# Last unit of expert weights in column halves: left columns first, then the right columns row by row

## The chip, the core and the metric

The kernel runs on one core of a Trainium2 chip. A core has five engines that run side by side: TensorE (PE) for matmuls, VectorE (DVE), ScalarE (ACT), GpSimd (POOL) and SyncE (SP), which here only issues transfers. Sixteen DMA engines move data between the chip's main memory and the core's on-chip memory of 128 partitions. TensorE writes its results into PSUM, eight banks of 512 float32 columns on 128 partitions. Engines wait for one another by semaphores. The metric is the time of one execution on the device in microseconds, here the median of the runs; less is better.

## What is computed

One layer of a decoder over 256 tokens of width 1024: attention and retention mixers side by side, their merge, then a mixture of 32 experts, of which each token uses 4, and a final norm. Only the experts' part matters here:

```python
def expert_block(args):
    tok, e = args
    xb = x_pad[tok]
    gu = xb @ w1[e] + b1[e]
    gate = jnp.minimum(gu[:, :F], SWIGLU_LIMIT)
    up = jnp.clip(gu[:, F:], -SWIGLU_LIMIT, SWIGLU_LIMIT)
    act = (up + 1.0) * gate * jax.nn.sigmoid(SWIGLU_ALPHA * gate)
    return act @ w2[e] + b2[e]
# y = expert output * gate weight, added to each token's row; then
return rmsnorm(x, norm_final_g)
```

w1 is 1024 x 2048 and w2 is 1024 x 1024 for each expert, in float32.

## The kernel before

The kernel loads every expert's weights once, all 32, and that is what most of the time goes to. The weights come in units of 2 MB: four units for w1 (two rows of 128 contracted values each, `W1_ROWS`) and two for w2 (four such rows each, `W2_ROWS`). A ring of ten places holds them. SP issues the loads in the order in which TensorE uses them, each when its place is free (`s_used` counts used units). Each unit's landing has a semaphore, and a transfer adds 16 to it when all 16 engines have done their part.

An expert has 64 slots for tokens (`CAP`). So each matmul of the experts has only 64 result rows, and the kernel puts two of them side by side: columns 0 to 511 of the result on partitions 0 to 63 of PSUM, columns 512 to 1023 on partitions 64 to 127. In `hidden_unit` (line 1241), `down_row` (line 1300) and `last_row` (line 1350) the loop over `c` goes through these halves. The halves of an expert's output are then brought back to token rows by `scatter_tile` (line 1390): for each tile of 128 tokens two matmuls, one that contracts partitions 0 to 63 (left columns) and one that contracts partitions 64 to 127 (right columns), added into banks 4 to 7, which hold the residual.

Weights and activations are float32, and such a matmul is two instructions of TensorE: the trace shows 32 of line 1350 for 16 matmuls. Each has its own weight load, which is listed under PEld.

The main loop handles 30 experts. The last two are written out: `hidden_last` for the hidden layer of expert 31 and `down_last` for the down projections of experts 30 and 31. There, three units of w2 are loaded in halves of two rows (line 574), and the last unit, the second of expert 31, in four quarters of one row (line 578), each with a semaphore of its own (`s_quarter`), so that TensorE can do a row when it has landed. The order on TensorE at the end is:

- rows 0 and 1 of expert 31's first unit of w2 (`down_halves(2, ...)`), then the scatter of token tile 1 of expert 30, then rows 2 and 3
- four rows of the last unit, each behind its own wait; the last adds to `s_used`
- `scatter_last`: the scatter of token tile 0 of expert 30, which needs nothing new, then, when DVE has copied expert 31's output from bank 1 of PSUM (line 1881, `main.ye`), tile 0 and tile 1 of expert 31. These two raise `s_first` and `s_scattered`.

ACT sums the squares of a token tile when these are raised (line 894) and takes the root (line 896); DVE inverts it and scales the tile (line 1907), and SP stores it in four pieces (line 593). Before that, DVE at the end does nothing but the copies from PSUM that the matmuls wait for. The routing of this input leaves no expert with more than 64 tokens, so the blocks for extra work (`If n > 0`) are not entered.

Of the kernel before, what the change touches and what calls it, by code (L numbers as in the profile page):

```python
# [16 lines left out]
P = 128  # L17
D = 1024
# [4 lines left out]
HALF = 512  # L23
# [14 lines left out]
CAP = 64  # L38
# [70 lines left out]
def hybrid_block_kernel(nc, x_in, g_mix, w_in, rel_bias, w_att, w_ret, w_out, g_ffn, w_router, b_router,  # L109
                        w1, b1, w2, b2, g_final, c_early, c_lasting, c_decay, c_onehot, c_mask, c_item,  # L110
                        c_expert, out):
    with ExitStack() as ctx:
# [3 lines left out]
        def sem(name):  # L116
            return ctx.enter_context(nc.semaphore(name))
# [257 lines left out]
        main, extra = Steps("main"), Steps("extra")  # L375
        s_w2half = [sem(f"last_w2_second_half_loaded{n}") for n in range(3)]
        s_first = sem("first_tile_scattered")

        s_unit = [sem(f"ring_unit_loaded{j}") for j in range(RING)]
        s_used = sem("ring_units_used")  # L380
# [14 lines left out]
        def w1_tile(flat):  # L395
            return flat.rearrange("p (j n) -> p j n", j=W1_ROWS)

        def w2_tile(flat):
            return flat.rearrange("p (j n) -> p j n", j=W2_ROWS)

        def w1_source(e, u):
            rows = W1_ROWS * P
            return w1[bass.ds(e, 1), u * rows:(u + 1) * rows, :].rearrange("e (p j) n -> p (e j) n", j=W1_ROWS)
# [11 lines left out]
        def w2_number(e, u):  # L415
            return W1_UNITS + E_UNITS * e + W1_UNITS + u if e < N_EXP - 1 else N_UNITS - W2_UNITS + u

        def place(n):
            in_halves = n >= RING and n % RING < HALF_UNITS
            return ring[n % RING], s_unit[n % RING], 16 * (n // RING + 1 + in_halves)  # L420

        def load_w1(sp, e, u, n):
            flat, landed, _ = place(n)
            sp.dma_start(w1_tile(flat), w1_source(e, u)).then_inc(landed, 16)

        def load_w2(sp, e, u, n):
            flat, landed, _ = place(n)
# [43 lines left out]
        def _(sp):  # L471
# [101 lines left out]
                    rows = slice(h * W2_ROWS // 2, (h + 1) * W2_ROWS // 2)  # L573
                    sp.dma_start(w2_tile(flat)[:, rows, :], w2_source(e, u)[:, rows, :]).then_inc(s_w2half[n] if h else landed, 16)
            sp.wait_ge(s_used, N_UNITS - 1 - RING + 1)
            for j in range(W2_ROWS):
                flat, _, _ = place(N_UNITS - 1)
                sp.dma_start(w2_tile(flat)[:, j, :], w2_source(N_EXP - 1, 1)[:, j, :]).then_inc(s_quarter[j], 16)  # L578

            sp.wait_ge(s_used, N_UNITS)  # L580
            sp.wait_ge(s_table, 1)
# [319 lines left out]
        def _(pe):  # L901
# [442 lines left out]
                        mm = row(flat, u * W2_ROWS + j)  # L1344
                mm.then_inc(s_used, 1)

            def last_row(flat, q):
                for c in range(2):
                    lhs = last_actT[:, (q % 4) * P + (q // 4) * CAP:(q % 4) * P + (q // 4) * CAP + CAP]
                    mm = pe.matmul(ps[CAP * c:CAP * c + CAP, 1, :], lhs,  # L1350
                                   w2_tile(flat)[:, q % W2_ROWS, c * HALF:(c + 1) * HALF],
                                   start=False, stop=(q == FQ - 1))
                return mm

            def down_last():
                i = N_EXP - 1
                down_bias(main, i - 1)
                down_halves(0, i - 1, 0, down_row)
                transpose_slots(main, i - 1)
                pe.wait_ge(main.act, i + 1)  # L1360
                for j in range(4):
                    mm = pe.transpose(ps[:, 0, j * P:(j + 1) * P], act_sb[:, j * P:(j + 1) * P], ident)
                mm.then_inc(main.at, 1)
                down_halves(1, i - 1, 1, down_row)
                pe.wait_ge(main.swe, i + 1)
                transpose_slots(main, i)
                pe.wait_ge(main.sel2, i + 1)
                pe.wait_ge(main.ate, i + 1)
                for c in range(2):
                    pe.matmul(ps[CAP * c:CAP * c + CAP, 1, :], sel2[0:BIAS_ROWS, :],  # L1370
                              bias[:, 2 * F + c * HALF:2 * F + (c + 1) * HALF], start=True, stop=False)
                down_halves(2, i, 0, last_row)
                flat, _, _ = place(w2_number(i, 1))
                for j in range(W2_ROWS):
                    pe.wait_ge(s_quarter[j], 32)
                    mm = last_row(flat, W2_ROWS + j)
                mm.then_inc(s_used, 1)

            def project_down_extra(i):
                down_bias(extra, i)  # L1380
                for u in range(W2_UNITS):
                    pe.wait_ge(s_extra2[u], i * 16 + 16)
                    down_unit(w2_part(u), u).then_inc(extra.w2_used, 1)
                    if u == 0:
                        transpose_slots(extra, i)

            def scatter_tile(t, weights, y):
                for c in range(2):
                    rows = slice(CAP * c, CAP * c + CAP)
                    mm = pe.matmul(bank(4 + 2 * t + c), weights[rows, t * P:(t + 1) * P], y[rows, :], start=False,  # L1390
                                   stop=True, skip_group_check=True)
                return mm

            def scatter(s, i):

# [4 lines left out]
                mm.then_inc(s_scattered, 1)  # L1400

            def scatter_last():
                scatter_tile(0, sc_w, y_sb)
                pe.wait_ge(main.ye, N_EXP + 1)
                pe.wait_ge(main.swe, N_EXP + 1)
                scatter_tile(0, last_sc, last_y).then_inc(s_first, 1)
                scatter_tile(1, last_sc, last_y).then_inc(s_scattered, 1)

            def second_scales():
                pe.wait_ge(main.slots, 2)  # L1410
# [43 lines left out]
        def _(dve):  # L1454
# [422 lines left out]
            store_y(main, N_EXP - 2)  # L1877
            dve.wait_ge(main.sw, N_EXP)
            dve.tensor_copy(last_sc, ps[:, 2, 0:T]).then_inc(main.swe, 1)
            dve.wait_ge(s_used, N_UNITS)  # L1880
            dve.tensor_copy(last_y, bank(1)).then_inc(main.ye, 1)
            n = dve.value_load(list_i[0:1, 0:1], min_val=0, max_val=MAX_EXTRA)
            with dve.If(n > 0):
                dve.wait_ge(s_scattered, N_EXP + 1)
# [54 lines left out]
```

## Time and profile before

| what | us |
|---|---|
| median of three runs | 1231.49 |
| lowest and highest | 1231.02, 1231.54 |
| the profiled execution | 1230.75 |
| its span, first to last instruction | 1228.7 |
| TensorE busy | 1168.7 (95%) |
| DVE busy, ACT busy | 427.1, 206.2 |
| moved by DMA | 462.31 MB, 376 GB/s in the mean |

The profile comes from one execution. Times in its rows count from the first instruction. A "busy" TensorE has at least one matmul in flight; its matmuls overlap, so the mean duration of one is longer than the distance from one to the next. The granted clock of TensorE was full throughout, but for the last slices behind its work.

### The profile page before, as it was taken

The page shows a single profiled execution, that of the slowest core. Times are in us where ns is not written, and L with a number is a line of the kernel's source. Part 1 is how long each engine was busy: PE and PEld are TensorE (multiplying, and loading weights), DVE is VectorE, ACT ScalarE, POOL GpSimd, SP SyncE. Part 2 cuts the span into 40 slices and gives each one's busy share as a digit, 9 for nine tenths or more (in the row PEclk, how much of TensorE's full clock was granted, in tenths as well). Part 3 has the DMA queues.
Part 4 walks back from the last instruction along what each step waited for, and adds up shares of the span by engine and source line. Part 5 has one row for each costly group of instructions (what it writes and reads, how often), then busy time and mean ns, then how long its engine had stood idle before and what let it go on. Part 6 is the DMA issues. An engine that isn't in the chain of part 4 may idle for free.

```text
span 1228.7 us, 17261 instructions
## 1 busy us (share of the span) xinstructions
PE 1168.7 (95%) x7138; PEld 584.6 (48%) x7138; DVE 427.1 (35%) x744; ACT 206.2 (17%) x303; POOL 58.6 (5%) x43
## 2 busy tenths in 40 slices
PE   9999999999999999999999999999999999899997
PEld 8888888888633333333333333333333333333332
DVE  5966765655722232222222222222222222222222
ACT  6444553534400000000000000000000000000001
POOL 0950000000300000000000000000000000000000
PEclk9999999999999999999999999999999999999999
DMA  9856437838999999999999999999999999999996
GB/s 312 267 207 224 152 137 269 310 140 350 409 428 427 429 428 428 428 429 428 429 428 428 429 428 428 428 428 429 429 428 428 429 428 429 428 429 429 428 425 281
DMA packets 57250, 462.31 MB, mean 376 GB/s; under 512 B 5761, under 2 KB 7490, under 8 KB 31906
## 3 DMA queue, kind: packets, MB, share of 16 engines
q1 hardware_dynamic: 53848, 458.97, 90.1%
q10 hardware_dynamic: 3370, 2.88, 0.8%
q8 instruction: 24, 0.39, 0.1%
q14 instruction: 8, 0.07, 0.0%
HBM read 459.71 MB, written 1.07 MB: 375 GB/s over the span
## 4 chain that ended last, share of the span: by engine, by line
PE 59%; DMA 37%; SPq 1%; ACT 1%; DVE 1%; issue 0%; DVEq 0%; ACTq 0%
DMA w_ring<-in_w 23%; PE ps L1241 15%; PE ps L1300 11%; DMA behind_watt<-in_w 7%; DMA behind_xb<-in_w 7%; PE ps L958 4%; PE ps L1390 3%; PE ps L966 3%; PE ps L964 3%; PE ps L965 3%; PE ps L1215 2%; PE ps L959 2%; SPq L578 1%; PE ps L978 1%; PE ps L1091 1%; PE ps L1093 1%
## 5 line engine op out<-in xcount | busy, mean ns | idle before, releaser
L1241 PE MATMUL ps<-w_ring,A_W 128*64 128x512 f32 x1232 | 278.1, 596 | 30.6 <-DMA w_ring<-in_w 29.1
L1830 DVE TENSOR_SCALAR A_W<-ps 128x512 f32<-128x512 f32 x32 | 22.1, 691 | 484.0 <-PE ps L1241 484.0
L1241 PEld LDWEIGHTS ps<-w_ring,A_W 128*64 128x64 f32 x1232 | 85.4, 137 | 205.8 <-issue 149.8
L1300 PE MATMUL ps<-w_ring,A_W 128*64 128x512 f32 x592 | 134.2, 595 | 0.0
L1472 DVE TENSOR_TENSOR w_parts<-w_ring,w_parts 128x1024 fp32r<-128x1024 f32 x76 | 110.0, 1466 | 57.2 <-ACT w_parts L690 56.3
L1241 PE MATMUL ps<-A_QK,A_W 128*64 128x512 f32 x416 | 94.2, 594 | 9.2 <-DMA A_QK<-in_w 8.7
L869 ACT ACTIVATE A_W<-ps 128x512 f32<-128x512 f32 x31 | 18.5, 597 | 438.3 <-PE ps L1281 438.3
L690 ACT ACTIVATE w_parts<-w_ring 128x1024 fp32r<-128x1024 f32 x75 | 78.9, 1058 | 64.7 <-PE ps L959 32.1
L865 ACT ACTIVATE A_W<-A_W 128x512 f32<-128x512 f32 x32 | 20.2, 630 | 394.8 <-DVE A_W L1830 394.8
L958 PE MATMUL ps<-hT_both,w_parts 128*128 128x512 f32 x224 | 79.3, 399 | 0.0
L1300 PEld LDWEIGHTS ps<-w_ring,A_W 128*64 128x64 f32 x592 | 40.4, 136 | 68.6 <-issue 66.9
L964 PE MATMUL ps<-w_parts,hT_both 128*128 128x512 f32 x176 | 69.6, 396 | 0.0
L966 PE MATMUL ps<-w_parts,hT_both 128*128 128x512 f32 x176 | 68.6, 390 | 0.0
L965 PE MATMUL ps<-w_parts,hT_both 128*128 128x512 f32 x176 | 68.5, 389 | 0.0
L1390 PE MATMUL ps<-A_W 64*128 64x512 f32 x264 | 65.9, 616 | 0.0
L959 PE MATMUL ps<-hT_both,w_parts 128*128 128x256 f32 x224 | 62.9, 281 | 0.0
L1241 PEld LDWEIGHTS ps<-A_QK,A_W 128*64 128x64 f32 x416 | 29.3, 137 | 70.4 <-issue 53.1
L1847 DVE COPY A_W<-ps 128x512 f32<-128x512 f32 x31 | 21.4, 692 | 98.2 <-PE ps L1300 98.2
L1241 PE MATMUL ps<-behind_watt,A_W 128*64 128x512 f32 x208 | 47.4, 597 | 5.4 <-DMA behind_watt<-in_w 5.0
L1241 PE MATMUL ps<-behind_xb,A_W 128*64 128x512 f32 x192 | 43.7, 597 | 5.5 <-DMA behind_xb<-in_w 5.0
L1215 PE MATMUL ps<-A_W,x_parts 128*128 128x64 bf16 x1488 | 48.5, 193 | 0.0
L958 PEld LDWEIGHTS ps<-hT_both,w_parts 128*128 128x128 f32 x224 | 42.1, 188 | 11.1 <-issue 0.6
(264 smaller groups left out, 1215.1 us busy)
## 6 DMA issues: line engine op xcount, KB each, us to landing
w_ring<-in_w SPq DMA_DIRECT2D x110, 2048.0 KB, 43.5
A_QK<-in_w SPq DMA_DIRECT2D x38, 2048.0 KB, 42.6
behind_watt<-in_w SPq DMA_DIRECT2D x19, 2048.0 KB, 43.5
w_ring<-in_w_in SPq DMA_DIRECT2D x36, 1024.0 KB, 7.4
behind_xb<-in_w SPq DMA_DIRECT2D x18, 2048.0 KB, 43.5
w_ring<-in_w SPq DMA_DIRECT2D x10, 1024.0 KB, 9.3
w_ring<-in_w_ret_branch SPq DMA_DIRECT2D x2, 2048.0 KB, 10.5
A_W<-in_w_out SPq DMA_DIRECT2D x1, 2560.0 KB, 13.2
```

The costliest lines, as they stand in the source:

```text
L690: act.activation(hi, raw, ACT.Copy).then_inc(s_wh, 1)
L958: pe.matmul(o, wh, tokens_both(k), start=first, stop=False, skip_group_check=True)
L959: mm = pe.matmul(o[:, 0, :], wl, hT_hi[:, k, :], start=False, stop=last, skip_group_check=True)
L964: pe.matmul(bank(b + t), hh, hi, start=first, stop=False)
L965: pe.matmul(bank(b + t), hh, lo, start=False, stop=False)
L966: mm = pe.matmul(bank(b + t), hl, hi, start=False, stop=last)
L1215: mm = pe.matmul(ps[:, 2, k * CAP:(k + 1) * CAP], x_part(part, t)[:, k * P:(k + 1) * P], s_one[:, t, :], start=(part == 0 and t == 0), sto ...
L1241: mm = pe.matmul(o, XT[:, k, :], tile[:, j, c * HALF:(c + 1) * HALF], start=(k == 0), stop=(k == KC - 1))
L1300: mm = pe.matmul(ps[CAP * c:CAP * c + CAP, 3, :], lhs, w2_tile(flat)[:, q % W2_ROWS, c * HALF:(c + 1) * HALF], start=False, stop=(q == FQ ...
L1390: mm = pe.matmul(bank(4 + 2 * t + c), weights[rows, t * P:(t + 1) * P], y[rows, :], start=False, stop=True, skip_group_check=True)
L1472: dve.tensor_tensor(lo, raw, hi.bitcast(F32), ALU.subtract).then_inc(s_wl, 1)
L1830: dve.tensor_scalar(gl, bank(0), LIMIT, None, ALU.min).then_inc(s.g, 1)
```

## The change

The last unit of w2 is still four transfers with four semaphores and the same 2 MB. They are now cut by columns first: the left 512 columns of all four rows (1 MB), then the right 512 columns of rows 0 and 1 (512 KB), of row 2 (256 KB) and of row 3 (256 KB). A partition's piece of a row is thus 2 KB where it was 4 KB.

TensorE does the left columns of all four rows behind the first landing and raises a new semaphore `s_left`. Then it does the scatter of tile 0 of expert 30, which stood behind the last row before. Then come the right columns of rows 0 and 1, and of row 2; the left scatter of expert 31's tile 0, which waits for DVE's copy of the left half; and the right columns of row 3. The sums of the right half go to bank 0 instead of bank 1, so that DVE can copy the left half out of bank 1 while TensorE writes the right one. DVE makes two copies of 64 partitions where it made one of 128. Behind the last row TensorE does the left scatter of tile 1, waits for the second copy, and does the right scatters of tile 0 and tile 1.

```diff
@@ load plan (SP)
+        LAST_PIECES = [(slice(0, W2_ROWS), slice(0, HALF)), (slice(0, 2), slice(HALF, D)),
+                       (slice(2, 3), slice(HALF, D)), (slice(3, 4), slice(HALF, D))]
...
-            for j in range(W2_ROWS):
-                flat, _, _ = place(N_UNITS - 1)
-                sp.dma_start(w2_tile(flat)[:, j, :], w2_source(N_EXP - 1, 1)[:, j, :]).then_inc(s_quarter[j], 16)
+            last_unit, last_source = w2_tile(place(N_UNITS - 1)[0]), w2_source(N_EXP - 1, 1)
+            for n, (rows, cols) in enumerate(LAST_PIECES):
+                sp.dma_start(last_unit[:, rows, cols], last_source[:, rows, cols]).then_inc(s_quarter[n], 16)
@@ TensorE
-            def last_row(flat, q):
-                for c in range(2):
+            def last_bank(c):
+                return ps[CAP * c:CAP * c + CAP, 1 - c, :]
+
+            def last_row(flat, q, columns=range(2)):
+                for c in columns:
                     lhs = last_actT[:, (q % 4) * P + (q // 4) * CAP:(q % 4) * P + (q // 4) * CAP + CAP]
-                    mm = pe.matmul(ps[CAP * c:CAP * c + CAP, 1, :], lhs,
-                                   w2_tile(flat)[:, q % W2_ROWS, c * HALF:(c + 1) * HALF],
+                    mm = pe.matmul(last_bank(c), lhs, w2_tile(flat)[:, q % W2_ROWS, c * HALF:(c + 1) * HALF],
                                    start=False, stop=(q == FQ - 1))
                 return mm
@@ down_last
+                pe.wait_ge(s_quarter[0], 32)
                 for j in range(W2_ROWS):
-                    pe.wait_ge(s_quarter[j], 32)
-                    mm = last_row(flat, W2_ROWS + j)
+                    mm = last_row(flat, W2_ROWS + j, (0,))
+                mm.then_inc(s_left, 1)
+                scatter_tile(0, sc_w, y_sb)
+                for n in range(1, 4):
+                    if n == 3:
+                        pe.wait_ge(main.ye, N_EXP + 1)
+                        pe.wait_ge(main.swe, N_EXP + 1)
+                        scatter_columns(0, 0, last_sc, last_y)
+                    pe.wait_ge(s_quarter[n], 32)
+                    rows = LAST_PIECES[n][0]
+                    for j in range(rows.start, rows.stop):
+                        mm = last_row(flat, W2_ROWS + j, (1,))
                 mm.then_inc(s_used, 1)
@@ scatter
+            def scatter_columns(t, c, weights, y):
+                rows = slice(CAP * c, CAP * c + CAP)
+                return pe.matmul(bank(4 + 2 * t + c), weights[rows, t * P:(t + 1) * P], y[rows, :], start=False,
+                                 stop=True, skip_group_check=True)
...
             def scatter_last():
-                scatter_tile(0, sc_w, y_sb)
-                pe.wait_ge(main.ye, N_EXP + 1)
-                pe.wait_ge(main.swe, N_EXP + 1)
-                scatter_tile(0, last_sc, last_y).then_inc(s_first, 1)
-                scatter_tile(1, last_sc, last_y).then_inc(s_scattered, 1)
+                scatter_columns(1, 0, last_sc, last_y)
+                pe.wait_ge(main.ye, N_EXP + 2)
+                scatter_columns(0, 1, last_sc, last_y).then_inc(s_first, 1)
+                scatter_columns(1, 1, last_sc, last_y).then_inc(s_scattered, 1)
@@ DVE
+            dve.wait_ge(s_left, 1)
+            dve.tensor_copy(last_y[0:CAP, :], ps[0:CAP, 1, :]).then_inc(main.ye, 1)
             dve.wait_ge(s_used, N_UNITS)
-            dve.tensor_copy(last_y, bank(1)).then_inc(main.ye, 1)
+            dve.tensor_copy(last_y[CAP:P, :], ps[CAP:P, 0, :]).then_inc(main.ye, 1)
```

## Rows read from the trace of the kernel before

**Rows 1.** The page: span, busy times, and DMA rate in 40 slices

```profile
span 1228.7 us, 17261 instructions
PE 1168.7 (95%) x7138; PEld 584.6 (48%) x7138; DVE 427.1 (35%) x744; ACT 206.2 (17%) x303; POOL 58.6 (5%) x43
GB/s 312 267 207 224 152 137 269 310 140 350 409 428 427 429 428 428 428 429 428 429 428 428 429 428 428 428 428 429 429 428 428 429 428 429 428 429 429 428 425 281
```

**Rows 2.** Chain that ended last, final stretch: start us, us, what

```profile
1194.79 23.71 DMA w_ring<-in_w
...
1218.54 1.08 PE ps L1350 x4
1219.62 1.95 PE ps L1390 x8
...
1221.59 1.12 ACT w_ring L894 x2
```

**Rows 3.** Timeline from 1210 on: start us, us, engine, line, operation [idle before]

```profile
1210.23 1.94 PE L1350 MATMUL ps<-w_ring,A_W 128*64 128x512 f32 x8
1212.10 1.13 PE L1390 MATMUL ps<-A_W 64*128 64x512 f32 x4
1213.16 4.51 PE L1350 MATMUL ps<-w_ring,A_W 128*64 128x512 f32 x20
1218.54 1.08 PE L1350 MATMUL ps<-w_ring,A_W 128*64 128x512 f32 x4 [0.87 <-DMA w_ring<-in_w]
1219.55 2.85 PE L1390 MATMUL ps<-A_W 64*128 64x512 f32 x12
1219.67 0.69 DVE L1881 COPY A_W<-ps 128x512 f32<-128x512 f32 x1 [8.91 <-PE ps L1350]
1220.41 0.30 PEld L1390 LDWEIGHTS ps<-A_W 64*128 64x128 f32 x4 [0.56 <-DVE A_W L1881]
1221.59 1.02 ACT L894 ACTIVATE w_ring<-ps 128x1024 f32<-128x1024 f32 x1 [13.20 <-PE ps L1390]
1222.94 1.00 ACT L894 ACTIVATE w_ring<-ps 128x1024 f32<-128x1024 f32 x1
```

**Rows 4.** Line 1350 in thin stretches, and its durations in ns (minimum, median, maximum)

```profile
core 0: us, PE busy (x) PEld busy (x), PEclk, DMA share, GB/s
1218.53:1218.56 0.03, 0.02 (x2) 0.02 (x2) 1.00 0.00 0
1218.56:1219.00 0.44, 0.44 (x2) 0.18 (x4) 1.00 0.00 0
1219.00:1219.04 0.04, 0.04 (x4) 0.00 (x0) 1.00 0.00 0
L1350 PE MATMUL ps<-w_ring,A_W x32: 592/592/644, 1210.2 to 1219.0; 128*64 128x512 f32 x32
```

**Rows 5.** Timeline: a matmul with no partner, and three on the whole array; durations of both

```profile
22.75 0.81 PE L1061 MATMUL ps<-A_W 32*12 32x384 f32 x2
L1061 PE MATMUL ps<-A_W x2: 481/484/488, 22.7 to 23.1; 32*12 32x384 f32 x2
124.51 1.46 PE L1005 MATMUL ps<-A_QK 128*128 128x256 f32 x6
L1005 PE MATMUL ps<-A_QK x24: 377/379/483, 124.5 to 171.3; 128*128 128x256 f32 x24
```

**Rows 6.** Line 578: issue durations in ns, starts, landing; output stores: KB each, landing

```profile
L578 SPq DMA_DIRECT2D w_ring<-in_w x4: 3932/4194/4239, 1182.3 to 1194.8; - x4
DMA to landing us min/median/max: 23.7/27.2/31.7
...
out<-xb SPq DMA_DIRECT2D x4, 256.0 KB, 2.0
```

**Rows 7.** DMA in three stretches: 224 to 228, 1212 to 1214, 1216 to 1217

```profile
DMA packets 805, 1.62 MB, mean 404 GB/s; under 512 B 16, under 2 KB 16, under 8 KB 805
...
DMA packets 225, 0.82 MB, mean 412 GB/s; under 512 B 24, under 2 KB 24, under 8 KB 225
...
q8 instruction: 1, 0.02, 6.7%
```

More of the change, by code:

```diff
@@ L377, in hybrid_block_kernel @@
         s_first = sem("first_tile_scattered")
+        s_left = sem("last_left_columns_done")
         s_unit = [sem(f"ring_unit_loaded{j}") for j in range(RING)]
@@ L1369, in down_last @@
                 for c in range(2):
-                    pe.matmul(ps[CAP * c:CAP * c + CAP, 1, :], sel2[0:BIAS_ROWS, :],
+                    pe.matmul(last_bank(c), sel2[0:BIAS_ROWS, :],
                               bias[:, 2 * F + c * HALF:2 * F + (c + 1) * HALF], start=True, stop=False)
@@ L1385, in project_down_extra @@
                         transpose_slots(extra, i)
+            def scatter_columns(t, c, weights, y):
+                rows = slice(CAP * c, CAP * c + CAP)
+                return pe.matmul(bank(4 + 2 * t + c), weights[rows, t * P:(t + 1) * P], y[rows, :], start=False,
+                                 stop=True, skip_group_check=True)
             def scatter_tile(t, weights, y):
[L1388 to L1392, printed above, removed]
+                scatter_columns(t, 0, weights, y)
+                return scatter_columns(t, 1, weights, y)
             def scatter(s, i):
```

## The prediction

> **What bounds the kernel now.** I read the page first [rows 1]. TensorE is busy for 95% of the span, the DMA engines move about 428 GB/s in nearly every slice of the second half, and only the last slice falls to 281. So the expert loop runs at the pace of the weights, and an edit at the very end can only touch what happens around the last landing. The change does not touch the bytes. Next I read the chain that ended last, over the final stretch [rows 2]. It is one long transfer, the last quarter of the last unit, issued at 1194.79 and landed 23.71 us later at 1218.50. Behind it come the last row of the down projection (from 1218.54), scatter matmuls (to 1221.57), and ScalarE's squares from 1221.59. From there to the end of the span at 1228.7 lie 7.1 us of ScalarE, VectorE and the stores, which the change leaves as they are. The question is thus when the first square can start: now it is at 1221.59, or 3.09 us after the last landing.
>
> Then I read the timeline of TensorE, DVE and ACT over that stretch [rows 3]. The reader should see that TensorE is not idle while the last unit lands. Its 20 instructions from 1213.16 run without a gap to 1217.67, and only then does it wait, for 0.87 us. They are the last two rows of the unit before and three of the four rows of the last unit. So before the change TensorE has work until 0.8 us ahead of the last landing, and there is not a whole row of slack. After the landing one row is left (x4, 1.08 us), the copy starts at 1219.67 and takes 0.69, and meanwhile TensorE does the first scatter tile of expert 30, which it had put off.
>
> **How fast the last matmuls can go.** This decides the sum. A row is two matmuls of 512 columns, one for the left half of the array's columns (partitions 0 to 63 of the result) and one for the right half, and each is two instructions. Line 1350 seen in thin slices [rows 4] shows the last row: two instructions begin together in the 0.03 us from 1218.53, none in the next 0.44 us, and two more at 1219.00. One instruction lasts 592 ns by the page's model but the next pair starts 0.43 us behind. So left and right run side by side, and one step of 0.43 us serves both. What does a half alone cost? A matmul with no partner is line 1061 [rows 5]: 384 columns, two instructions, 0.81 us for both, each 484 ns, so the second starts 0.33 us after the first. That is 0.44 for 512 columns by proportion. Line 1005, on the whole array, says the same: six instructions of 256 columns in 1.46 us with a last one of 0.38 make 0.216 us each, or 0.43 for 512. So a half alone takes the full 0.43 us a step, and a step with one half does half the work.
>
> Two more prices from [rows 3]. Where rows and scatter matmuls follow one another, something is added: the block of 8 at 1210.23 has four steps (1.72) and the next starts 1.87 later, so 0.15 is added; the scatter block at 1212.10 has two steps (0.86) and the next starts 1.06 later, so 0.20.
>
> **The transfers.** The last unit's four issues begin between 1182.3 and 1194.8, and they take 23.7 to 31.7 us to land [rows 6]. The first is the slowest, 1182.3 + 31.7 = 1214.0. A quarter of 512 KB at 412 GB/s [rows 7] takes 1.27 us, so the half unit before it landed at 1212.7. The change makes the first piece 1 MB in packets of 2 KB instead of 4. Projection weights come in such packets: 805 packets carried 1.62 MB in 4 us at 404 GB/s [rows 7]. So the left half lands 2.60 us later, at 1215.3, and the smaller packets cost 2% (0.1 us over the unit). Its ends: 2.45 us at the loop's 428 GB/s, and 0.7 us more if the piece is held up as the last quarter is now (1214.0 + 3 x 1.27 = 1217.8, but it landed at 1218.50; beside it one 16 KB packet of the instruction queue ran [rows 7]). The right pieces need 2.6 us more, until 1217.9, or 1218.6 with that hold-up. SP's four issues now carry twice the packets. SP already waits about 4.2 us in each for room, and was done with the last at 1199, 16 us before its data moved, so more waiting there is hidden; if that cover went, each microsecond of a late issue would land 1:1 in the end.
>
> **The change on TensorE, block by block.** The two rows of the unit before are ready at 1213.16 and done by 1214.9, as now. The engine then waits for all the left rows at once, where it used to start on the first quarter at once behind them.
> - Left rows, from 1215.32: four matmuls of one half, 8 steps, 3.44 + 0.15. Next block at 1218.91. Before, four rows with both halves would take these same 8 steps.
> - First scatter tile of expert 30, moved here from behind the last row: 2 steps, 1.06, to 1219.97. It was hidden beside the DVE copy; now it lies in the path.
> - Right rows 0 to 2: 6 steps, 2.58 + 0.15, to 1222.70. Their weights landed long before, so the waits cost nothing.
> - Left scatter of tile 0: 2 steps with half of the array's rows idle, 1.06, to 1223.76. Its wait is for the left copy: the left sums are ready about 1219.1 and DVE needs 0.69, so by 1219.9. DVE had been idle 8.91 us at that point, and nothing is queued behind the wait that is due earlier.
> - Right row 3: 2 steps. As now, the copy starts 1.13 after the row's start (1218.54 to 1219.67): 1224.89. The copy of 64 partitions still has 512 columns; I take 0.69, bounded below by half of that. The next weight load follows 0.74 after its start, 1220.41 now, 1225.63 then. Left scatter of tile 1 stands before it, from 1224.77 to about 1225.7, hidden by the copy (0.1 us if not).
> - Right scatter of tile 0: 2 steps. Now the two steps of tile 0 start at 1219.55 + 0.53 + 0.43 = 1220.51 and ACT follows 1.08 later. So ACT starts at 1225.63 + 1.08 = 1226.71.
> - Right scatter of tile 1 ends 0.86 later. ACT wants it 1.35 after its first square (1221.59 to 1222.94), so it costs nothing.
>
> The sum: 1226.71 - 1221.59 = +5.12 us. The profiled execution took 1230.75 us, of which 1228.7 are the span. It becomes 1235.9. The median of the runs is 1231.49, 0.74 more than the profiled one, and becomes 1236.6.
>
> Where does it come from? Counted from 1213.16, TensorE had 10 steps before it waited for the last landing, and two after. Now 8 left, 8 right and 2 scatter steps stand ahead of the last copy, behind a wait that ends at 1215.3. The last landing is no longer late at all: the right columns lie ready for several microseconds. What the change could give is small besides: with TensorE idle at the last landing, the last row still takes two steps and the copy 0.69, and the scatter behind it starts at 1220.41 instead of 1220.51. That is 0.1 us.
>
> **The rivals.**
> - *Half matmuls cost half.* If the engine ran the two instructions of one matmul side by side, a step of a half would be 0.215 us. Then the left rows end at 1217.2 (8 x 0.215 + 0.15), the scatter tile at 1218.25, right rows 0 to 2 at 1219.7, the left scatter at 1220.3; the copy starts at 1221.0 and ACT at 1222.4: +0.8, or 1232.3, which is within 0.2%. This is the case on the other side: not slower. There are 20 half steps in the path, so it decides at 0.43 - (5.12 - 2.46)/20 = 0.30 us a step. Against it are lines 1061 and 1005 [rows 5]. For it is only that the pairs of [rows 4] do not say which two instructions they are. 6%.
> - *Right rows slip past.* In [rows 4] the two that start together cannot be neighbours in the program if those of line 1061 run one behind the other: a right instruction overtakes a left one. If right rows 0 and 1 could also start beside the left ones, 1.87 us go, and the time is 1234.7. Against it: the scatter tile stands between and needs all columns of the array. 7%. The Trainium skill (TensorE: Matmul & The Clock Gate, Part 3, What overlaps and what doesn't) has matmuls in strict order with no reordering; by it this rival is nil, but the trace's pairs speak against the rule, so I leave it a chance. The same part's Measured speedup vs the span model gives 2.38 for three column tiles, not 3; by that ratio two tiles give 1.59, a step of one half would be an estimated 0.34 us, and the sum about +3.4, an estimated 1234.9. The trace's 0.33 for 384 columns disagrees.
> - *The left piece is late.* All of TensorE's chain hangs on one landing now. With the hold-up of 0.7 the time is 1237.3. If the piece pays besides for a start of its own, bounded by the output stores, 256 KB in 2.0 us [rows 6] of which 0.65 is data at 404 GB/s, it is 1.35: 1238.0. Against: the quarters land with no pause between them [rows 7]. 9%.
> - *It does not do what it says.* The left copy and its scatter are to run while the right columns land. By my times the right columns are in by 1218.6 and the left sums are ready at 1219.1, so nothing overlaps with landing. This is part of the forecast, and of the rival where halves cost half it is the opposite.
> - *The landing gets earlier.* If the instruction packet no longer meets the last piece and TensorE keeps up, the end moves by -0.7 - 0.1, to 1230.7. TensorE does not keep up even in the first rival, so this gets 1%, and even it is within 0.2%.
>
> **How the numbers follow.** Forecast 75%, 1236.6, itself within 1236.0 to 1237.2. Slipping 7%, late 9%, halves at half price 6%, landing 1%, anything else 2% (half of it faster). The range from 1234.6 to 1238.0 takes in the forecast, slipping and the late piece. A difference of 0.2% (2.5 us) is about what a measurement of this kernel can tell from no change. Faster 0.01, same 0.08, slower 0.91.
>
> **What would show it.** In the profile after, line 1350's counterpart with one half must show 8 instructions in some 3.6 us from about 1215.3, with one begun at a time, 0.43 us apart; TensorE must have no idle time for a DMA after that; the last DVE copy must start near 1224.9 and the first square near 1226.7. The chain that ended last must run through TensorE from about 1215 on. A wait of TensorE for the last piece would make the prediction wrong, and so would left rows done within 2 us.

## The result, and the profile after

The changed kernel takes 1236.36 us in the median of six runs (1236.05 to 1238.18), the kernel before 1231.3 us (1230.76 to 1231.86, six runs). The ratio is 1.0043, with a 95% interval from 1.0033 to 1.0054. So it is slower by 5.06 us. The forecast was 1236.6, 5.1 us slower.

The profiled execution took 1236.55 us with a span of 1234.3. The one before took 1230.75 with 1228.7; it lay 0.55 below the median of its kernel and this one 0.19 above, so the two profiles are 5.8 us apart where the medians are 5.06. The page first. The bytes are the same, 462.31 MB, and so are the busy times of all engines but TensorE within 1.2 us. The rates of the first ten slices differ from [rows 1] by up to 21 GB/s either way, from the 11th to the 39th they agree within 2. Only the last slice is clearly lower, because it has more time without transfers.

```profile
span 1234.3 us, 17262 instructions
PE 1173.8 (95%) x7138; PEld 585.4 (47%) x7138; DVE 428.3 (35%) x745; ACT 206.3 (17%) x303; POOL 58.4 (5%) x43
GB/s 314 264 205 233 141 137 286 309 121 371 407 426 428 427 426 430 427 429 427 430 427 428 430 426 430 427 430 427 430 428 428 429 427 430 427 430 427 429 424 205
```

TensorE has the same 7138 matmul instructions and is busy 5.1 us longer. The chain that ended last (start, length, what) shows where. In [rows 2] a transfer ran until 1218.50, and behind it were one row and eight scatter instructions. Here the transfer in the chain is the first piece, landed at 1215.67, and all the rest up to ScalarE is TensorE:

```profile
1181.87 33.80 DMA w_ring<-in_w
...
1215.71 3.65 PE ps L1357 x8
1219.36 1.06 PE ps L1406 x4
1220.42 2.72 PE ps L1357 x6
1223.14 1.05 PE ps L1406 x2
1224.19 1.00 PE ps L1357 x2
1225.19 1.92 PE ps L1406 x4
...
1227.14 1.12 ACT w_ring L898 x2
```

Line 1357 is `last_row` (1350 before), line 1406 the scatter matmul (1390 before), lines 1899 and 1901 the two copies. The timeline answers to [rows 3]. The reader should see the eight instructions of the left rows taking 3.65 us, as long as sixteen take in pairs (the run with the transfers alone, below, shows that), and that no matmul behind them waits for a transfer; the last line is the weight load that waits for the second copy:

```profile
1213.44 1.94 PE L1357 MATMUL ps<-w_ring,A_W 128*64 128x512 f32 x8
1215.71 3.65 PE L1357 MATMUL ps<-w_ring,A_W 128*64 128x512 f32 x8 [0.34 <-DMA w_ring<-in_w]
1219.29 1.13 PE L1406 MATMUL ps<-A_W 64*128 64x512 f32 x4
1219.39 0.68 DVE L1899 COPY A_W<-ps 64x512 f32<-64x512 f32 x1 [8.37 <-PE ps L1357]
1220.35 2.79 PE L1357 MATMUL ps<-w_ring,A_W 128*64 128x512 f32 x6
1223.07 1.12 PE L1406 MATMUL ps<-A_W 64*128 64x512 f32 x2
1224.12 1.07 PE L1357 MATMUL ps<-w_ring,A_W 128*64 128x512 f32 x2
1225.23 0.69 DVE L1901 COPY A_W<-ps 64x512 f32<-64x512 f32 x1 [5.15 <-PE ps L1357]
1225.98 0.29 PEld L1406 LDWEIGHTS ps<-A_W 64*128 64x128 f32 x2 [0.56 <-DVE A_W L1901]
```

Thin stretches of line 1357 answer to [rows 4]. Where two instructions began together every 0.43 us, now one does (x1, then x2 while the former still runs):

```profile
1215.70:1215.72 0.02, 0.01 (x1) 0.01 (x1) 1.00 0.26 102
1215.72:1216.18 0.46, 0.46 (x1) 0.18 (x2) 1.00 0.70 267
1216.18:1216.20 0.02, 0.02 (x2) 0.01 (x1) 1.00 0.29 103
1216.20:1216.61 0.41, 0.41 (x2) 0.13 (x1) 1.00 0.52 200
```

### The profile page after: what moved, and what is told of

Read it like the earlier page. It is cut to its first block, busy times and chain, and to the rows that moved or that the text cites. A ratio compares the mean times of both kernels' runs of the same rounds, so it can differ in the third digit from the quotient of the medians.

```text
span 1234.3 us, 17262 instructions
## 1 busy us (share of the span) xinstructions
PE 1173.8 (95%) x7138; PEld 585.4 (47%) x7138; DVE 428.3 (35%) x745; ACT 206.3 (17%) x303; POOL 58.4 (5%) x43
## 2 busy tenths in 40 slices
DMA packets 57762, 462.31 MB, mean 375 GB/s; under 512 B 5761, under 2 KB 7490, under 8 KB 32418
## 4 chain that ended last, share of the span: by engine, by line
PE 60%; DMA 38%; ACT 1%; DVE 1%; issue 0%; SPq 0%; DVEq 0%; ACTq 0%
DMA w_ring<-in_w 24%; PE ps L1245 15%; PE ps L1304 11%; DMA behind_watt<-in_w 7%; DMA behind_xb<-in_w 7%; PE ps L962 4%; PE ps L1406 3%; PE ps L970 3%; PE ps L969 3%; PE ps L968 3%; PE ps L1219 2%; PE ps L963 2%; PE ps L982 1%; PE ps L1095 1%; PE ps L1096 1%; PE ps L1097 1%
```

## The experiments

Two theories were set against each other. Theory A is that of the prediction: a row of one column half takes the full 0.43 us a step, TensorE falls behind, and all that follows the left landing is one chain of TensorE. Theory B: the transfers in column pieces cost the time. The runs were made in three groups, each beside the kernel before on the same chip, and a time is set against the kernel before of its own group. The first group has the changed kernel again, the order alone, the partner and the left piece in two (kernel before: 1231.39 us). The second has the transfers alone, the scatter in the gap and the first version with 256 columns (1231.35). The third has the last two (1231.26).

**The changed kernel again.**

> The changed kernel once more, on the chip of the next three, so that they can be compared with it: +5.0 to +5.3 us over the kernel before, the first square of ScalarE at about 1227.1 in the profile. Theory A (a row of one column half takes the full 0.43 us a step, so TensorE is the bound from the left landing on) and theory B (the transfers in column pieces of 2 KB packets are late and hold the end up) both expect just this.

Measured: 1236.48 us (1236.37 to 1238.52, four runs), 5.09 more than the kernel before, ratio 1.0045 (1.0029 to 1.0062), first square at 1227.16. As expected.

**The order alone.** The changed kernel with the old transfers:

```diff
-            for n, (rows, cols) in enumerate(LAST_PIECES):
-                sp.dma_start(last_unit[:, rows, cols], last_source[:, rows, cols]).then_inc(s_quarter[n], 16)
+            for j in range(W2_ROWS):
+                sp.dma_start(w2_tile(flat)[:, j, :], w2_source(N_EXP - 1, 1)[:, j, :]).then_inc(s_quarter[j], 16)
...
-                pe.wait_ge(s_quarter[0], 32)
                 for j in range(W2_ROWS):
+                    pe.wait_ge(s_quarter[j], 32)
                     mm = last_row(flat, W2_ROWS + j, (0,))
```

> Order of TensorE and copies of the changed kernel, but the last unit comes in four quarters by rows as before, packets of 4 KB. Theory A: nothing is gained by the old transfers. Left rows 0 to 2 start as the quarters land, from 1214.9; left row 3 waits for the last quarter at 1218.5 and is over with 1.01 us later, so the scatter tile starts at 1219.55 against 1219.29 in the changed kernel: +5.3 us over the kernel before, 0.3 more than the changed one. Theory B: the time goes back to that of the kernel before, within 0.5 us.

Measured: 1236.94 us (1236.84 to 1237.22, four runs), ratio 1.0044 (1.0027 to 1.0061). The median is 0.46 above that of the changed kernel, with ranges that overlap, and the profile agrees: the scatter tile begins 0.47 later (1219.76 for 1219.29; expected 0.3). Its timeline has the left rows 0 to 2 in one block with the pairs before them (x14, 4.50 us), then the fourth behind the last landing:

```profile
1213.41 4.50 PE L1357 MATMUL ps<-w_ring,A_W 128*64 128x512 f32 x14
1218.76 1.07 PE L1357 MATMUL ps<-w_ring,A_W 128*64 128x512 f32 x2 [0.85 <-DMA w_ring<-in_w]
1219.76 1.13 PE L1405 MATMUL ps<-A_W 64*128 64x512 f32 x4
```

The old transfers bring nothing back. Theory B is out as the cause of the 5 us.

**The transfers alone.** The kernel before with the four pieces of the change; TensorE does each row with both halves when its right piece has landed:

```diff
+                pe.wait_ge(s_quarter[0], 32)
+                for n in range(1, 4):
+                    pe.wait_ge(s_quarter[n], 32)
+                    for j in range(LAST_PIECES[n][0].start, LAST_PIECES[n][0].stop):
+                        mm = last_row(flat, W2_ROWS + j)
-                for j in range(W2_ROWS):
-                    pe.wait_ge(s_quarter[j], 32)
-                    mm = last_row(flat, W2_ROWS + j)
```

> The kernel before with the transfers of the change alone: left columns of the last unit first, then the right ones in three pieces. TensorE does each row with both halves side by side, as before, behind the landing of its right piece. Theory A: rows 0 and 1 wait for the second piece, about 1217.0, and then 8 steps run without a gap (3.44 us), so the copy starts at about 1220.7 where it was 1219.7: +1.0 us over the kernel before. Theory B: about the +5 us of the changed kernel.

Measured: 1232.04 us against 1231.35, ratio 1.0005 (0.9996 to 1.0014). The medians differ by 0.7, and the interval does not tell it from no change. The transfers are worth at most some 1.7 us (the interval's upper end) and, by the medians, 0.7. The timeline says how they cost anything: TensorE waits 1.66 us with nothing to do, since it can't begin a row before its right piece, and then has eight steps in a row.

```profile
1217.86 3.65 PE L1353 MATMUL ps<-w_ring,A_W 128*64 128x512 f32 x16 [1.66 <-DMA w_ring<-in_w]
```

In 3.65 us it does sixteen instructions. The changed kernel does eight in the same 3.65.

**A partner beside each left row.** This measures the disputed cost by itself. The changed kernel, with four matmuls added that use the idle half of the array and write to a bank that nobody reads:

```diff
+            def partner(flat, q):
+                lhs = last_actT[:, (q % 4) * P + (q // 4) * CAP:(q % 4) * P + (q // 4) * CAP + CAP]
+                return pe.matmul(ps[CAP:P, 3, :], lhs, w2_tile(flat)[:, q % W2_ROWS, 0:HALF], start=True, stop=True)
...
-                    mm = last_row(flat, W2_ROWS + j, (0,))
+                    last_row(flat, W2_ROWS + j, (0,))
+                    mm = partner(flat, W2_ROWS + j)
```

> The changed kernel with four matmuls more: beside each left row of the last unit one of the right column half of the array, of the same size, from weights that have landed, into a bank that nobody reads. Theory A: the other half of the array is idle there, so the 8 added instructions are nearly free, the block of left rows stays at 3.6 to 3.7 us and the time within 0.2 us of the changed kernel. If a half matmul costs by its work, the block grows by 1.7 us and the time with it.

Measured: 1236.74 us (1236.12 to 1237.45), ratio 1.0043 (1.0027 to 1.006), not told from the changed kernel's 1236.48. The left rows begin at 1215.55 and the scatter at 1219.14, 3.59 us later; in the changed kernel it is 3.58 (1215.71 to 1219.29). Line 1363 is the partner, and each begins 0.01 us behind a left one (shown are the first two pairs of eight and the scatter):

```profile
1215.55 0.64 PE L1357 MATMUL ps<-w_ring,A_W 128*64 128x512 f32 x1 [0.34 <-DMA w_ring<-in_w]
1215.56 0.64 PE L1363 MATMUL ps<-w_ring,A_W 128*64 128x512 f32 x1
1216.03 0.59 PE L1357 MATMUL ps<-w_ring,A_W 128*64 128x512 f32 x1
1216.04 0.59 PE L1363 MATMUL ps<-w_ring,A_W 128*64 128x512 f32 x1
...
1219.14 1.13 PE L1411 MATMUL ps<-A_W 64*128 64x512 f32 x4
```

Eight more instructions of full size cost 0.01 us. Half of the array was idle through the left rows. That is theory A, measured.

**The left piece in two.** Does the end hang on the left landing?

```diff
+                if n == 0:
+                    for h, landed in enumerate((s_quarter[0], s_left2)):
+                        two = slice(2 * h, 2 * h + 2)
+                        sp.dma_start(last_unit[:, two, cols], last_source[:, two, cols]).then_inc(landed, 16)
+                    continue
...
+                    if j == 2:
+                        pe.wait_ge(s_left2, 16)
                     mm = last_row(flat, W2_ROWS + j, (0,))
```

> The changed kernel with the left piece cut in two transfers of two rows each, so that left rows 0 and 1 need not wait for rows 2 and 3. Theory A: all behind the left landing is one chain of TensorE, so the end moves 1:1 with its start. The first two rows land at about 1214.3, TensorE is free at 1214.9 and goes on without a wait: 0.8 us less than the changed kernel, +4.3 over the kernel before. Theory B (the last landings decide): no change against the changed kernel, as the last bytes land as late.

Measured: 1236.18 us, ratio 1.0039 (1.0025 to 1.0053), 0.3 less than the changed kernel, with ranges that overlap. The profile is clearer. The block runs on without a wait, and the scatter tile begins at 1218.79 instead of 1219.29, as the span ends 0.5 earlier (1233.8 for 1234.3).

```profile
1213.49 5.36 PE L1363 MATMUL ps<-w_ring,A_W 128*64 128x512 f32 x16
1218.79 1.13 PE L1414 MATMUL ps<-A_W 64*128 64x512 f32 x4
```

So it moves 1:1, as expected, but by 0.5 and not 0.8. The 0.8 was my mistake: I had TensorE free at 1214.9, as in the kernel before, while in the profiles of the changed kernels it begins these rows 0.3 later (1213.44 and 1213.49, where [rows 3] have 1213.16).

**The halves side by side in time.** The scatter tile of expert 30 that stood between left and right rows is moved up, beside the other one. Then left and right rows are neighbours, in different halves of the array. It tests the rival that right rows slip past, and at the same time takes the tile out of the chain:

```diff
                         pe.wait_ge(main.ye, N_EXP)
+                        scatter_tile(0, sc_w, y_sb)
                         scatter_tile(1, sc_w, y_sb).then_inc(s_scattered, 1)
...
                 mm.then_inc(s_left, 1)
-                scatter_tile(0, sc_w, y_sb)
```

> The changed kernel with the first scatter tile of expert 30 moved up beside the second one, before the left columns. So nothing stands between the left rows and right rows 0 to 2 of the last unit, and they use different halves of the array. It tells whether TensorE takes right instructions beside left ones out of the order of the program. Theory A with strict order between matmuls: left start goes from 1215.7 to about 1216.1, then 8 + 6 steps one behind the other, 6.2 us, and 1.06 us of scatter with its switch are gone from the path: 0.8 us less than the changed kernel, +4.3 over the kernel before. Theory A with slipping: right rows 0 to 2 run beside left rows as soon as they have landed (1217 to 1217.7), both blocks together take some 3.6 to 4.5 us, and the time is 2.4 to 3.4 us less than the changed kernel's, +1.7 to +2.7 over the kernel before.

Measured: 1233.76 us against 1231.26, ratio 1.0021 (1.0012 to 1.003). That is +2.5 us, half of what the change costs, and inside what slipping would give. The chain has one block of 22 instructions, four pairs and then left and right rows, in 6.21 us, and the first square comes at 1224.18:

```profile
1213.98 6.21 PE ps L1358 x22
1220.19 1.05 PE ps L1406 x2
...
1224.18 1.12 ACT w_ring L898 x2
```

The four pairs take 1.77 of it, and the 14 instructions of left and right rows 4.4 us, a little over ten steps instead of fourteen. Thin stretches show the slip. At first one instruction runs and one begins, then in 0.02 us at 1217.38 two begin (x3: two and the one still running), and from there on four are seen in each short stretch, which is two running and two beginning:

```profile
1216.97:1217.38 0.41, 0.41 (x2) 0.13 (x1) 1.00 0.18 60
1217.38:1217.40 0.02, 0.02 (x3) 0.01 (x2) 1.00 0.03 0
...
1217.81:1217.89 0.08, 0.08 (x4) 0.07 (x2) 1.00 0.00 0
```

The left rows are eight instructions from 1215.67, so at 1217.39 the fifth of them begins, and three more stand ahead of every right one in the program. The right ones begin beside them all the same. The weight loads show it too, and so does the left copy (line 1899), which waits for the last left instruction. It starts at 1219.31, and the trace has that last left instruction from 1218.68 on, when three right ones had begun:

```profile
1216.96 0.14 PEld L1358 LDWEIGHTS ps<-w_ring,A_W 128*64 128x64 f32 x1 [0.29 <-issue]
1217.39 0.19 PEld L1358 LDWEIGHTS ps<-w_ring,A_W 128*64 128x64 f32 x3 [0.29 <-issue]
1217.82 0.20 PEld L1358 LDWEIGHTS ps<-w_ring,A_W 128*64 128x64 f32 x2 [0.23 <-issue]
...
1219.31 0.68 DVE L1899 COPY A_W<-ps 64x512 f32<-64x512 f32 x1 [8.66 <-PE ps L1358]
```

The first square comes at 1224.18 and not at 1227.14: 2.96 us, of which four saved steps are 1.72, and the scatter block and its switch nearly all of the rest (1.06 + 0.15). The right piece was there before: the landing events of the trace have it at 1216.58. Why the first pair forms only 0.8 us later isn't settled, but the trace has a hint. At 1216.96, with the piece landed, a left instruction still begins alone, and four left ones are ahead of the first right one. At 1217.39 three are ahead, and it joins. So the engine may look only a few instructions ahead. This bears on the changed kernel: there the scatter tile, four instructions, stands between the last left instruction and the first right one. Whether the tile keeps right rows from slipping past because it needs the whole array, or only because it puts them too far back, no run here tells. A run with four instructions on left columns alone in place of the tile would.

**Scatter in the gap.** The kernel before, with the scatter tile put where TensorE waits for the last quarter:

```diff
                 for j in range(W2_ROWS):
+                    if j == W2_ROWS - 1:
+                        scatter_tile(0, sc_w, y_sb)
                     pe.wait_ge(s_quarter[j], 32)
...
             def scatter_last():
-                scatter_tile(0, sc_w, y_sb)
```

> The kernel before, with the first scatter tile of expert 30 put between rows 2 and 3 of the last unit, where TensorE waits 0.87 us for the last quarter. Theory A: it takes 1.06 us from 1217.5 to 1218.56, hardly later than the landing at 1218.5, and frees TensorE when the copy is done (1220.41 against 1220.51): -0.1 us, which can't be told from no change by the times. If moving it into the path were itself costly, +1 us.

Measured: 1231.39 us against 1231.35, ratio 0.9999 (0.999 to 1.0008). The tile did hold row 3 up: its quarter had landed at 1218.97 by the trace's landing events, and it began at 1219.28, where the kernel before begins 0.04 behind the landing.

```profile
1218.22 1.13 PE L1392 MATMUL ps<-A_W 64*128 64x512 f32 x4
1219.28 1.08 PE L1350 MATMUL ps<-w_ring,A_W 128*64 128x512 f32 x4
```

TensorE now idles 0.79 us for the copy, but from the start of the copy to the first square it is 1.93 us (1220.40 to 1222.33) where it was 1.92 (1219.67 to 1221.59). The 0.1 us that I counted on is lost again: from the first of the two steps to the square it is 1.18 us (1221.15 to 1222.33), where it was 1.08 with TensorE at work before them. From the last landing to the first square this profile has 3.35 us, the kernel before 3.09. The medians show nothing of it.

**Columns cut without splitting the pairs.** If the pairs are what matters, columns can be cut inside each half: matmuls of 256 columns, left and right still side by side, the first 256 of each into bank 1, the rest into bank 0. DVE copies the first part while TensorE does the second. Transfers are as before.

```diff
+            def last_row(flat, q, parts=range(2)):
+                for h in parts:
+                    for c in range(2):
+                        at = c * HALF + h * T
+                        mm = pe.matmul(ps[CAP * c:CAP * c + CAP, 1 - h, 0:T], lhs,
+                                       w2_tile(flat)[:, q % W2_ROWS, at:at + T], start=False, stop=(q == FQ - 1))
...
+                    if j == W2_ROWS - 1:
+                        last_row(flat, W2_ROWS + j, (0,)).then_inc(s_left, 1)
+                        mm = last_row(flat, W2_ROWS + j, (1,))
...
+            dve.wait_ge(s_left, 1)
+            dve.tensor_copy(last_y[:, 0:T], ps[:, 1, 0:T]).then_inc(main.ye, 1)
             dve.wait_ge(s_used, N_UNITS)
+            dve.tensor_copy(last_y[:, T:2 * T], ps[:, 0, 0:T]).then_inc(main.ye, 1)
```

The scatters of expert 31 are cut at 256 columns in the same way, and the first version has the scatter tile in the gap as above.

> A version that overlaps copy and matmuls without giving up the pairs: the scatter tile early as in the run before, every row of expert 31 in matmuls of 256 columns, both array halves side by side, the first 256 columns of each half into bank 1 and the others into bank 0. The transfers are those of the kernel before. Behind the last landing DVE copies the first columns while TensorE does the others, and scatters them while DVE copies the rest. Theory A: a step of 256 columns takes 0.215 us, so from the landing at 1218.5 the first copy starts at 1219.25 (0.42 us), the second at 1219.7, the last scatter steps at 1220.15, and ScalarE at 1220.8: -0.7 us against the kernel before. If each of the smaller matmuls costs more than its columns, no gain or a loss.

Measured: 1231.47 us against 1231.35, ratio 1.0002 (0.9993 to 1.0011). No gain, and the chain shows why: the scatter tile (line 1400) now lies in it ahead of the last row.

```profile
1217.53 1.08 PE ps L1353 x8
1218.61 1.06 PE ps L1400 x4
1219.67 0.61 PE ps L1353 x4
...
1220.78 1.16 PE ps L1416 x8
...
1221.96 1.12 ACT w_ring L895 x2
```

Row 2 began only at 1217.53, when its quarter had landed (1217.48, a microsecond later than in the kernel before), so there was no gap of a microsecond, and the last row started at 1219.60, 0.87 behind its landing at 1218.73. From 1219.60 to the first square it is 2.36 us, 0.69 less than the 3.05 of the kernel before (1218.54 to 1221.59): this is what I expected. The overlap works, and the tile in the wrong place took it back. The late quarter itself has no tested cause: by the landing events the second quarter took 2.19 us here and the last 1.25, where in the kernel before the second took 1.29 and the last 2.01, so the hold-up fell on another piece.

**The same with the tile beside the other one.** Between the pairs of the unit before, where the switch from rows to scatter is paid anyway:

```diff
                         pe.wait_ge(main.ye, N_EXP)
+                        scatter_tile(0, sc_w, y_sb)
                         scatter_tile(1, sc_w, y_sb).then_inc(s_scattered, 1)
...
-                    if j == W2_ROWS - 1:
-                        scatter_tile(0, sc_w, y_sb)
```

> The version with matmuls of 256 columns once more, but the scatter tile of expert 30 stands beside the other one and not between rows 2 and 3, where it held row 3 up by 0.87 us and so took back what the overlap gave. Both tiles together take 0.86 us more and no further switch, and TensorE ends row 2 at about the time of the last landing (1218.4 to 1218.7). From the start of row 3 to ScalarE's first square: 2.36 us, as in the run before, against 3.05 in the kernel before. So -0.5 to -0.7 us against the kernel before, 0.05%, which shows in the profile and hardly in the times. If TensorE is late on row 3 again by more than 0.3 us, no gain.

Measured: 1230.62 us (1230.4 to 1231.67, 11 runs) against 1231.26 (1230.51 to 1231.9, 21 runs), ratio 0.9997 (0.9988 to 1.0006). The medians are 0.64 us apart, as expected; the interval doesn't tell it from no change. In the profile the last row starts right behind its landing (1218.98), and the first square comes 2.36 us after that start. From the landing to the first square it is 2.41 us, where the kernel before has 3.09.

```profile
1195.27 23.71 DMA w_ring<-in_w
...
1219.03 0.68 PE ps L1354 x4
...
1219.73 0.44 DVE A_W L1900
...
1220.21 1.16 PE ps L1415 x8
...
1221.39 1.12 ACT w_ring L895 x2
```

## Why the prediction was right, point by point

- *TensorE has work until the last landing, and half steps cost as much as whole ones.* Right. The eight left steps took 3.58 us to the next block (forecast 3.59), one instruction begun every 0.43. The partner run shows that the other half of the array was free for as much work again.
- *The blocks.* Counted from the left start to the first square, the forecast was 1226.71 - 1215.32 = 11.39 us and the profile has 1227.14 - 1215.71 = 11.43. The scatter tile took 1.06, right rows 0 to 2 2.72 (forecast 2.73), the left scatter 1.05, row 3 to the copy 1.11 (1.13). The second copy of 64 partitions took 0.69, the same as one of 128; the lower bound of half of it is not reached. One count beside the sum is short: I wrote that 2 scatter steps stand ahead of the last copy. My own list and the profile have 4 (line 1406, x4 in two steps and x2 in two steps); the sum holds all of them.
- *The left landing.* Forecast 1215.3, it was 1215.67. Of the 0.4, about 0.3 lie in all of this profile around there: TensorE begins the rows of the unit before at 1213.44 instead of 1213.16. The packets of 2 KB are left with 0.1: from the landing of the half unit before, the left piece took 2.70 us here and 2.67 to 2.71 in the four other profiles with such a piece, two quarters 2.55 to 2.56 in the kernel before and two of its variants. The hold-up of 0.7 that one rival had did not come. Without the 0.28 by which all is later, the first square moved by 5.27 us, where the sum had 5.12. The medians moved by 5.06. That the median was hit to 0.24 us (1236.36 for 1236.6) is in part luck: the profiled execution missed its forecast of 1235.9 by 0.65, and six runs of the kernel before spread over 1.1.
- *The transfers are worth little.* Right in the changed kernel, where TensorE hides the right pieces. By themselves, with rows in pairs, they showed 0.7 us in the medians, less than the 1.0 that I expected and not told from zero. The kernel with the old transfers and the new order was not faster than the changed one.
- *SP's issues are hidden.* Right: the last now begins at 1203.4 instead of 1194.8, still long before its data move.

```profile
L582 SPq DMA_DIRECT2D w_ring<-in_w x4: 4012/4430/13112, 1181.9 to 1203.4; - x4
```

- *The copy and the scatter do not overlap with the landing.* Right: the left copy starts at 1219.39, and the stretch from 1218 to 1220 shows 0 GB/s.

```profile
1218.00:1220.00 2.00, 2.00 (x8) 0.48 (x6) 0.60 (x1) 0.00 (x0) 0.00 (x0) 1.00 0.00 0
```

- *The rivals.* "Half matmuls cost half" is out by the partner run. "Right rows slip past" did not happen in the changed kernel, but it does happen with the scatter tile out of the way: right rows run beside left ones, and 1.72 us come back. So the forecast was right on the outcome, and the reason that I gave, that the tile between needs all columns of the array, fits but is not shown: a reach of a few instructions would do the same. I wrote that the pairs of [rows 4] did not say which two instructions they are; the run with the halves adjacent shows a left and a right one pair, since they are there far apart in the program. The strict order that the Trainium skill states (TensorE: Matmul & The Clock Gate, Part 3, What overlaps and what doesn't) does not hold in that trace; the measurement decides.

In the changed kernel the 5 us thus come from two things. Of the 5.5 us in the profiles (1227.14 - 1221.59), 2.96 go when the scatter tile no longer stands between left and right rows: 1.2 for the tile itself, 1.7 for the slipping that does not happen with it there. That is a measured difference of two kernels, 2.6 in the medians (+5.06 less +2.50). The tile is not gone in that run; it stands ahead of the left rows, where the changed kernel waits for the left piece. The rest, 2.6 us (2.5 in the medians), stays.

What the rest is made of I read from the timelines and did not test piece by piece. Against the kernel before there are four more row steps (1.72), because eight half steps find no partner: the first four of the left ones, before the right rows join, two of the right ones behind them, and two of row 3. The left scatter block has its own place in the chain (1.05). The moved tile of expert 30, which in the kernel before ran beside the copy, stands ahead of the rows (0.86). Against that, the 0.87 us in which TensorE waited for the last quarter are used up. Together that is 2.76, where the profiles have 2.59 (1224.18 - 1221.59).

## What to carry to other kernels

Where two small matmuls share the array, their pairing is worth a factor of two (sixteen instructions or eight in the same 3.65 us), and an order that puts all of one half first gives it away. Cut inside each half instead, so that a piece still has a partner; here that gave 0.64 us in the medians, which the interval doesn't tell from nothing, and 0.69 us from row 3 to the first square in the profile. A finer cut pays only on an engine that would otherwise wait. Before moving work ahead of a last landing, count how much time the engine has there; TensorE had 0.87 us. And look for what stands between two blocks that could overlap: moving one scatter tile out from between them was worth half of the loss.

## What the runs showed of the hardware

- Matmuls in different column halves of the array do not keep the order of the program. With the halves adjacent, the first right instruction began at 1217.40, while three left ones that stand ahead of it had not begun. How far this reaches, and what stops it, is open.
- Eight full-size matmul instructions beside others in the free half cost 0.01 us (3.59 against 3.58 us, the partner run).
- Where row matmuls and scatter matmuls alternate, a block took 0.14 to 0.20 us more than its steps of 0.43 us, in all the traces looked at (3.58 us for 8 steps, 1.06 for 2).
- A copy out of PSUM of 64 partitions takes as long as one of 128 (0.68 and 0.69 us against 0.69), while one of half the columns takes 0.42 to 0.44.
